# Expert items of a mixture layer run as big, small, big, small to the end, with overflow items in pairs behind them

## The reference

```python
def moe(h, router, w_gate_up, w_down):
    xt = h.reshape(B * S, D)                                  # 256 x 1024
    probs = jax.nn.softmax((xt @ router), axis=-1)            # 8 experts
    top_p, top_i = lax.top_k(probs, TOP_K)                    # 2 of 8
    top_p = top_p / jnp.sum(top_p, axis=-1, keepdims=True)
    gates = jnp.sum(one_hot(top_i, 8) * top_p[..., None], axis=1)
    y = jnp.zeros_like(xt)
    for e in range(N_EXPERTS):
        y = y + gates[:, e:e+1] * swiglu(xt, w_gate_up[e], w_down[e])
    return y
def swiglu(h, w_gate_up, w_down):                             # 1024 x 5632, 2816 x 1024
    g, u = jnp.split(h @ w_gate_up, 2, axis=-1)
    return (jax.nn.silu(g) * u) @ w_down
```

## Time and profile before

| | |
|---|---|
| Time, median of 3 | 1169.89 us (1169.28 to 1170.38) |
| Profiled execution, its time | 1167.88 us |
| Profiled execution, span | 1166.0 us |
| PE busy | 1089.2 us, 93% |
| DVE busy | 625.4 us, 54% |
| ACT busy | 522.0 us, 45% |
| Read from memory | 341.37 MB, 294 GB/s over the span |
| TensorE clock granted, mean | 0.979 of full |

### The profile page before, as it was taken

One profiled execution on the slowest core, in us unless ns is written; L12 is line 12 of the kernel. 1 busy time (PEld: TensorE's weight loads), 2 busy tenths in 40 slices (PEclk: granted clock), 3 DMA queues, 4 the chain that ended last, 5 costly groups with the idle time before them and its releaser, 6 DMA issues.

```text
span 1166.0 us, 15739 instructions
## 1 busy us (share of the span) xinstructions
PE 1089.2 (93%) x5708; PEld 800.3 (69%) x5708; DVE 625.4 (54%) x693; ACT 522.0 (45%) x571; POOL 22.5 (2%) x93
## 2 busy tenths in 40 slices
PE   7899999999999988999999999999998999999774
PEld 7867788888898777787446786446787788443131
DVE  6755555555654448895108894008886997301002
ACT  5544544344445644773016773016775676110001
POOL 2100000000000000000000000000000000000000
PEclk9889999999999999999999999999999999999998
DMA  9932455555454424997999999999999999799995
GB/s 353 335 108 86 165 184 184 177 186 211 145 182 147 140 73 146 370 361 270 379 409 409 400 410 396 391 409 410 400 409 367 343 361 357 287 403 409 406 403 202
DMA packets 122455, 343.47 MB, mean 295 GB/s; under 512 B 12893, under 2 KB 39562, under 8 KB 122378
## 3 DMA queue, kind: packets, MB, share of 16 engines
q1 hardware_dynamic: 122234, 341.94, 78.5%
q10 hardware_dynamic: 144, 0.52, 0.1%
HBM read 341.37 MB, written 1.05 MB: 294 GB/s over the span
## 4 chain that ended last, share of the span: by engine, by line
PE 75%; SPq 9%; DVE 5%; DMA 4%; issue 3%; ACT 3%; POOL 0%; POOLq 0%; DVEq 0%; ACTq 0%
PE ps L1454 19%; PE ps L1455 19%; PE ps L1456 19%; PE ps L1459 16%; SPq L361 5%; SPq L365 4%; DMA raw<-moe_w_gate_up_dram 3%; ACT whi L547 1%; DMA raw<-moe_w_down_dram 1%; DVE wlo L948 1%; PE ps L1789 1%; PE ps L1469 1%; DVE h L1131 1%; DVE wlo L937 0%; ACT xs L547 0%
## 5 line engine op out<-in xcount | busy, mean ns | idle before, releaser
L547 ACT ACTIVATE whi<-raw 128x2048 fp32r<-128x2048 f32 (+1 forms) x195 | 335.8, 1725 | 241.2 <-PE ps L1456 231.2
L948 DVE TENSOR_TENSOR wlo<-raw,whi 128x2048 fp32r<-128x2048 f32 x151 | 345.8, 2293 | 123.1 <-ACT whi L547 121.3
L1454 PE MATMUL ps<-whi,xhi 128*128 128x512 f32 (+3 forms) x688 | 265.7, 386 | 13.9 <-DVE wlo L948 5.1
L1455 PE MATMUL ps<-whi,xlo 128*128 128x512 f32 (+3 forms) x688 | 261.7, 380 | 0.0
L1456 PE MATMUL ps<-wlo,xhi 128*128 128x512 f32 (+3 forms) x688 | 261.3, 380 | 0.0
L1459 PE MATMUL ps<-raw,xs 128*64 128x512 f32 (+2 forms) x1024 | 158.5, 462 | 10.5 <-DMA raw<-moe_w_gate_up_dram 10.4
L1454 PEld LDWEIGHTS ps<-whi,xhi 128*128 128x128 f32 x688 | 131.1, 190 | 41.9 <-DVE wlo L948 7.4
L1456 PEld LDWEIGHTS ps<-wlo,xhi 128*128 128x128 f32 x688 | 130.9, 190 | 24.2
L1455 PEld LDWEIGHTS ps<-whi,xlo 128*128 128x128 f32 x688 | 130.9, 190 | 22.5
L1459 PEld LDWEIGHTS ps<-raw,xs 128*64 128x64 f32 x1024 | 67.1, 137 | 98.2 <-issue 65.6
L1454 PE MATMUL ps<-whi,hhi 128*128 128x512 f32 x264 | 106.5, 403 | 0.0
(11 more groups left out here) (282 smaller groups left out, 973.9 us busy)
## 6 DMA issues: line engine op xcount, KB each, us to landing
raw<-moe_w_gate_up_dram SPq DMA_DIRECT2D x256, 512.0 KB, 12.2
raw<-moe_w_down_dram SPq DMA_DIRECT2D x176, 512.0 KB, 14.0
raw<-moe_w_gate_up_dram SPq DMA_DIRECT2D x96, 384.0 KB, 9.5
raw<-ffn_w_gate_up_dram SPq DMA_DIRECT2D x44, 512.0 KB, 4.9
raw<-ffn_w_down_dram SPq DMA_DIRECT2D x22, 512.0 KB, 4.0
raw<-kv_shared_w_dram SPq DMA_DIRECT2D x16, 512.0 KB, 3.7
raw<-moe_w_gate_up_dram SPq DMA_DIRECT2D x32, 256.0 KB, 9.8
raw<-mla_w_o_dram SPq DMA_DIRECT2D x8, 512.0 KB, 14.0
```

The costliest lines, as they stand in the source:

```text
L547: return nc.scalar.activation(o, i, ACT.Copy, scale=scale)
L948: V.tensor_tensor(wlo[:, s, :].rearrange("p a w -> p (a w)"), raw[:, (hh // 2) % RAW, :], whi[:, s, :].bitcast(F32).rearrange("p a w -> p ...
L1454: pe.matmul(o, a_hi, b_hi, start=start, stop=False, skip_group_check=True)
L1455: pe.matmul(o, a_lo, b_hi, start=False, stop=False, skip_group_check=True)
```

## The change

The items now alternate to the end: B S B S B S B S. `PAIRS` becomes 4. Two pairs are still in straight code, then a loop over pairs follows, and the last pair is written out behind it. If there are overflow items, they follow in further pairs of one big and one small item; ITEMS grows from 13 to 14 rows. The number of further pairs, and which expert stands where in them, is worked out by DVE in a longer row of tiny operations. What an item does is unchanged, and so are its slots and which experts are small.

```diff
-NB = N_EXP - NS
-PAIRS = 2
-OVF = 5
-FIRST_OVF = 6
-LATE = FIRST_OVF + OVF
-ITEMS = LATE + 2
-ORDER = (0, 1, 5, 2, 6, 7) + OVF * (-1,) + (3, 4)
+PAIRS = N_EXP - NS
+OVF = 6
+FIRST_OVF = 2 * PAIRS
+ITEMS = FIRST_OVF + OVF
+ORDER = (0, 1, 5, 2, 6, 3, 7, 4) + OVF * (-1,)
...
             sp_eng.wait_ge(items_ready, 2)
-            for p in range(PAIRS):
+            for p in range(PAIRS - 2):
                 small_loads(p, at(2 * p + 1), lambda x: after_big(x, p))
                 big_loads(p + 1, at(2 * p + 2), lambda x: after_small(x, p))
-            final = sp_eng.value_load(final_i[0:1, 0:1], min_val=NB - 1, max_val=NB - 1 + OVF)
-            with sp_eng.Fori(PAIRS + 1, final + 1) as i:
-                big_loads(i, at(i + PAIRS), lambda x: after_big(x, i - 1))
-            small_loads(PAIRS, at(LATE), lambda x: after_big(x, final))
-            small_loads(PAIRS + 1, at(LATE + 1), lambda x: after_small(x, PAIRS))
+            final = sp_eng.value_load(final_i[0:1, 0:1], min_val=PAIRS - 1, max_val=PAIRS - 1 + OVF // 2)
+            with sp_eng.Fori(PAIRS - 2, final) as p:
+                small_loads(p, at(2 * p + 1), lambda x: after_big(x, p))
+                big_loads(p + 1, at(2 * p + 2), lambda x: after_small(x, p))
+            small_loads(final, at(2 * final + 1), lambda x: after_big(x, final))
...
-            for p in range(PAIRS):
+            for p in range(PAIRS - 2):
                 big(p, 2 * p, "small", p)
                 small(p, 2 * p + 1, "big", p + 1)
             pe.wait_ge(items_ready, 2)
-            final = pe.value_load(final_i[0:1, 0:1], min_val=NB - 1, max_val=NB - 1 + OVF)
-            with pe.Fori(PAIRS, final) as i:
-                big(i, i + PAIRS, "big", i + 1)
-            big(final, final + PAIRS, "small", PAIRS)
-            small(PAIRS, final + PAIRS + 1, "small", PAIRS + 1)
-            small(PAIRS + 1, final + PAIRS + 2, None, None)
+            final = pe.value_load(final_i[0:1, 0:1], min_val=PAIRS - 1, max_val=PAIRS - 1 + OVF // 2)
+            with pe.Fori(PAIRS - 2, final) as p:
+                big(p, 2 * p, "small", p)
+                small(p, 2 * p + 1, "big", p + 1)
+            big(final, 2 * final, "small", final)
+            small(final, 2 * final + 1, None, None)
```

ACT and DVE get the same loop, and POOL's runs over the same number of items. In the routing, seven instructions on DVE (lines 1390 to 1396) become twenty:

```diff
+            V.tensor_scalar(cap2[:, :], place[:, :], 0.5, None, ALU.is_gt)
+            step(V.tensor_scalar(wide[:, :], place[:, :], NS + 0.5, None, ALU.is_gt))
+            step(V.tensor_tensor(wide[:, :], cap2[:, :], wide[:, :], ALU.is_equal))
+            step(V.tensor_scalar(cap[:, :], wide[:, :], -float(P - SMALL), -float(SMALL), ALU.mult, ALU.add))
             step(V.tensor_tensor(ovf[:, :], cnt[:, :], cap[:, :], ALU.add))
             step(V.tensor_scalar(ovf[:, :], ovf[:, :], 0.0, None, ALU.is_gt))
+            step(V.tensor_tensor(wide[:, :], wide[:, :], ovf[:, :], ALU.mult))
+            step(V.tensor_tensor(cap2[:, :], ovf[:, :], wide[:, :], ALU.subtract))
+            V.tensor_tensor_scan(csum[:, :], ones[:, 0:N_EXP], wide[:, :], 0.0, ALU.mult, ALU.add)
+            step(V.tensor_tensor_scan(csum2[:, :], ones[:, 0:N_EXP], cap2[:, :], 0.0, ALU.mult, ALU.add))
...
+            step(V.tensor_tensor(csum[:, :], csum[:, :], cap2[:, :], ALU.add))
...
-            V.tensor_scalar(final_i[:, :], csum[:, N_EXP - 1:N_EXP], float(NB - 1), None, ALU.add).then_inc(items_ready, 1)
+            V.tensor_scalar(final_i[:, :], extra[:, 2:3], float(PAIRS - 1), None, ALU.add).then_inc(items_ready, 1)
```

More of the change, by code:

```diff
@@ L208, in build @@
             ("sp", [P, HEADS, 384], F32))
-        lg, lg2, oh1, oh2, sc8, msk, gates, posn, posc, ovf, csum, key, place, cap, cap2, less, order, oh, prod, \
+        lg, lg2, oh1, oh2, sc8, msk, gates, posn, posc, ovf, csum, key, place, cap, cap2, wide, csum2, extra, less, order, oh, prod, \
             m1, m2, den, best, rank, cnt, tf, xr = over(
@@ L901, in _ @@
             act.wait_ge(items_ready, 2)
[L902 to L910, removed]
+            final = act.value_load(final_i[0:1, 0:1], min_val=PAIRS - 1, max_val=PAIRS - 1 + OVF // 2)
+            with act.Fori(PAIRS - 2, final) as p:
+                big(p, 2 * p, "small")
+                small(p, 2 * p + 1, "big")
+            big(final, 2 * final, "small")
+            small(final, 2 * final + 1, None)
+            n_items = 2 * final + 2
             for c in range(TC):
@@ L1204, in add_in, with big @@
                                                op0=ALU.mult, op1=ALU.add).then_inc(h_ready[4], 1)
-            def big(i, g, row, following, next_row):
+            def big(i, g, following):
                 def gate(j):
@@ L1226, in big @@
                     if x == 14:
-                        item_gates(g, row)
-                        choose(g + 1, next_row, following)
+                        item_gates(g)
+                        choose(g + 1, following)
                     if x == FU - 1:
@@ L1243, in big, with small @@
                 add_in(g)
-            def small(p, g, row, following, next_row):
+            def small(p, g, following):
                 def gate(j):
@@ new lines, in _ @@
+            step(V.tensor_scalar(extra[:, 2:3], n_narrow, 2.5, None, ALU.is_gt))
+            step(V.tensor_tensor(extra[:, 1:2], extra[:, 1:2], extra[:, 2:3], ALU.add))
+            V.tensor_tensor(extra[:, 1:2], extra[:, 1:2], n_wide, ALU.max)
+            step(V.scalar_tensor_tensor(out=cap2[:, :], in0=csum2[:, :], scalar=extra[:, 0:1], in1=csum2[:, :],
+                                        op0=ALU.mult, op1=ALU.add))
+            V.scalar_tensor_tensor(out=extra[:, 2:3], in0=n_narrow, scalar=extra[:, 0:1], in1=extra[:, 1:2],
+                                   op0=ALU.mult, op1=ALU.max)
@@ L1427, in _ @@
                 split_low_unit(H_MOE + 2 * x)
-            for p in range(PAIRS):
-                big(p, 2 * p, 2 * p, "small", 2 * p + 1)
-                small(p, 2 * p + 1, 2 * p + 1, "big", 2 * p + 2)
+            for p in range(PAIRS - 2):
+                big(p, 2 * p, "small")
+                small(p, 2 * p + 1, "big")
             dve.wait_ge(items_ready, 2)
-            final = dve.value_load(final_i[0:1, 0:1], min_val=NB - 1, max_val=NB - 1 + OVF)
-            with dve.Fori(PAIRS, final) as i:
-                big(i, i + PAIRS, i + PAIRS, "big", i + PAIRS + 1)
-            big(final, final + PAIRS, final + PAIRS, "small", LATE)
-            small(PAIRS, final + PAIRS + 1, LATE, "small", LATE + 1)
-            small(PAIRS + 1, final + PAIRS + 2, LATE + 1, None, None)
-            n_items = final + PAIRS + 3
+            final = dve.value_load(final_i[0:1, 0:1], min_val=PAIRS - 1, max_val=PAIRS - 1 + OVF // 2)
+            with dve.Fori(PAIRS - 2, final) as p:
+                big(p, 2 * p, "small")
+                small(p, 2 * p + 1, "big")
+            big(final, 2 * final, "small")
+            small(final, 2 * final + 1, None)
+            n_items = 2 * final + 2
             dve.wait_ge(gbc_in, 16)
```

32 lines of the change are left out of this document (16 added, 16 removed).

## The result

| | before | after |
|---|---|---|
| Time, median of 4 | 1169.74 us (1169.28 to 1170.38) | 1151.6 us (1151.32 to 1153.6) |
| Ratio, with its 95% interval | | 0.9848 (0.9831 to 0.9865) |
| Profiled execution, its time (span) | 1167.88 (1166.0) us | 1151.79 (1150.0) us |
| PE, DVE, ACT busy | 1089.2, 625.4, 522.0 us | 1085.4, 627.3, 522.4 us |
| Read from memory | 341.37 MB | 341.37 MB |

The account below looks back on a forecast made before the run. PE was taken to bound the kernel, with S3 slowed by an emptied weight ring. Terms -18.4 and +0.5 gave -17.9 from the profiled 1167.88: 1150.0, plus 2.0 for the median, 1152.0 us; range 1147.5 to 1158.

Parts of the forecast that it names:

- Steps 1 and 3: Mixture stretches: S2, moved behind a big item, takes 62.2 us; B2 and B3 take 110.96 us each, as B1 did.
- step 3: Handovers between items: B2 and B3 together take 221.92 us against 216.93 before, a cost of 5.0 us.
- step 2: Last small item, S3, with no next gather: 62.3 us, bounds 58.5 and 75, its end set by the last unit's landing.
- step 4: The mixture behind S1's end: 346.4 us in place of 364.84, so 18.4 us less.
- signs named: Profile after: S3 62 us with hardly any PE waits for transfers, last `ys` at some 1134.5, B0's first product at most 1 us late.
- step 5: Longer DVE routing ahead of B0: partly absorbed by DVE's idle time, delaying PE's first product by 0 to 0.8 us, taken as 0.5.
- step 6: Loops on each engine, with computed waits and addresses: no cost, at most 0.5 us a handover, 1 us in all.
- The ring is not refilled: Rival, chance 0.09: later pairs run slower in transfers, so S2 and S3 begin with fewer units: 1158 to 1164 us.
- The transfers bind throughout: Rival, chance 0.03 (no change): S3's wait comes back in pieces before S2, B3 and S3: 1170 us.
- SP's issue as a bound: Rival, chance 0.03 (slower): SP's issue of computed transfers for S2 and B3 becomes the bound: 1178 to 1193 us.
- More is gained: Rival, chance 0.05: the last item's missing gather counts in full and transfers keep S0's state: 1147 to 1149 us.

Follow-up runs that it names:

- e1: The kernel after with its items in the order B B S S B S B S: 1172.16 us, ratio 1.0005 to the kernel before.
- e2: The kernel before with the order B B B B S S S S: 1209.75 us, ratio 1.0335.
- e9: The kernel before with each weight transfer of the last small item half as wide, same computing: 1146.37 us, ratio 0.9793 to the kernel before.
- e10: The kernel after with each weight transfer of the last small item half as wide, same computing: 1146.51 us, ratio 0.9794 to the kernel before.
- e3: The kernel after with thirteen of the added DVE instructions of the routing taken out again: 1152.43 us, ratio 0.9856 to the kernel before.
- e6: The kernel after with the loop written out on all five engines and a fixed number of rounds: 1152.88 us, ratio 0.9843 to the kernel before.
- e5: The kernel after with a gather, its result thrown away, put back into the last small item: 1151.74 us, ratio 0.9842 to the kernel before.
- e11: The kernel after, PE taking three units of the following small item behind the big item's ninth down unit and two more in `begin`: 1144.49 us, ratio 0.9791.
- e7: The kernel after with 2.1 MB more transfers per small item, ahead of its units 2 and 8, while the big item runs: 1163.21 us, ratio 0.9939.
- e8: The kernel after with 2.1 MB more transfers per small item, ahead of its units 18 and 24, while the small item runs: 1170.61 us, ratio 1.0003.
- e4: The kernel after with 24 more DVE instructions in the routing, each waiting for the one before: 1157.82 us, ratio 0.9896 to the kernel before.

## Why the prediction was right

I forecast 1152.0 us, in a range from 1147.5 to 1158; it was 1151.6, by the mechanism named.

**Steps 1 and 3 held as numbers.** S2 was put at 62.2 and took 62.05. B2 and B3 were put at 110.96 each and took 110.95 and 111.04. e1, e2 and e9 show that the reading behind them is the cause, and not only fits it: the loss goes with the place behind a small item, comes once for each such place, and vanishes with the last item's transfers.

**But they are right only together.** The prediction says of the four small items that PE's work in them is the same. In the stretches as cut it is not: S3 before holds 363 products and S3 after 345, while B2 and B3 together hold 987 before and 1006 after. The 24 us between 85.97 and 62 contain the 4.8 of PE's work that e9 and e10 price, and the 5.0 of step 3 is not a cost of handovers but this work on the other side of the cuts. The empty ring cost 18 to 20 us, not 24. Both steps went by the same cuts, so the sum came out right.

**S3 (step 2)** was the one term that was mis-sized: 62.3 forecast, 62.97 measured, and 63.1 to 64.5 in e1 and e3 to e6. The argument from the last landing was right, as the five units at 2.55 and e5 show, but I took S1's landing for S3's. That S3's last unit lands at the end of a pair with little slack, so that each small delay of the transfers ahead arrives there, would explain the spread; no run separates it.

**The sum (step 4)**: 18.4 less behind S1's end was forecast, 17.83 measured. The missing 0.6 is S3's. Two of the signs named did not come out as written: the last `ys` is at 1136.56 and not some 1134.5, and PE still waits 4.3 us for transfers in S3.

**The routing (step 5)** was put at 0.5. Counted from `rt_cnt` it is 0.56 at PE's transposes, and 0.42 at the end of B0 (554.37 less 439.75, against 552.36 less 438.16). `final_i` came 2.08 later, and the idle time of DVE behind it took 1.4 of this, much as the step said: where the earlier trace rows have 1.15 and 0.66 of waiting, after has 0 and 0.38. From the end of the kernel after's routing:

```profile
445.62 0.15 DVE L1419 TENSOR_SCALAR final_i<-rt_extra 128x1 int32<-128x1 f32 x1
445.68 1.12 DVE L1172 SCALAR_TENSOR_TENSOR xlo<-ps,gcol,xhi 128x128 fp32r<-128x128 f32 x4
447.18 1.13 DVE L1172 SCALAR_TENSOR_TENSOR xlo<-ps,gcol,xhi 128x128 fp32r<-128x128 f32 x4 [0.38 <-ACT xhi L545]
```

What the prediction did not have is that `rt_cnt` itself is 1.59 later in the profiled execution of after. That is not of the change, since the code ahead of it is the same: by 225 us (a group of `h` in the dense layer) 1.47 of it was there (226.43, not 224.96), with a granted clock of 0.86 from 50 to 100 us where it had been 0.90, and e3 to e6, e10 and e11 have this group at 225.2 to 226.8. With 0.42 from the routing and 0.17 won in S0 to S1 it makes the 1.84 at S1's end. It also puts the transposes ahead of B0 2.15 later in the trace, past the 1 us that the prediction allowed, though the change accounts for 0.56 of it. So single executions differ by some 1.5 us ahead of the mixture, and the profiled difference (16.1) is 2.0 below that of the medians (18.1). My number for the profiled execution, 1150.0, was 1.8 too low; the 2.0 that I had added for the median made up for it, since after was profiled at its median (1151.79 and 1151.6) and before was not. That the forecast is within 0.4 us is luck to this extent.

**The loops (step 6)** were put at nothing, and the stretches of e6 show nothing.

**The rivals.** *The ring is not refilled* did not happen, but of the two arguments for and against it the wrong one decided. I held SP's 14.7 us of waiting for DVE against it, and e7 shows that this waiting is no room. The slack of 1.5 us in a pair, which I had worked out from the lengths, was the right one: e7 finds 0.6 to 1.7. The rival's mechanism was nearer than its chance of 0.09 says: e7, with 5.2 us more of transfers for each small item, took the 1158 to 1164 that I had given for it. *The transfers bind throughout* falls with the result; e8 shows what it would have looked like. *SP's issue as a bound* falls: S2 and B3 took what S1 and B2 took, and SP still waited 14.7 to 18.1 us for slots. *More is gained* falls for the reason that e5 gives.

On bandwidth the prediction quoted one figure of the Trainium skill too narrowly. "DMA: Bandwidth & Descriptors" gives 358 GB/s in its Specifications, but says under Measured that this is the share of a core when both cores of a pair stream, and "Perfetto Trace Analysis" (Roofline) adds that one core alone is bounded by its DMA engines at some 435. This kernel runs on one core, and the items from S0 to B3 show 395 to 404 GB/s, up to 408 in e7, so the second statement agrees with the trace and the rival drawn from the first was none.

## What to carry to other kernels

Cut the timeline at the ends of like pieces of work and put length and GB/s side by side: a piece that is slow only in one place of the order, next to a piece that moves less than full pace, is a case for exchanging the two. "Perfetto Trace Analysis" of the Trainium skill (Optimization Strategy) says the same of stretches with different limits, that they may gain from being interleaved; here, with a buffer of a third of an item, each small item behind a small one cost 18 to 20 us. Look at what lies on either side of a cut before you give a difference to a wait: two stretches of the same item can hold different work. Read the room of the transfers from GB/s against the highest seen, in pieces of a few us, and not from the sum of the issuing engine's waits; then, when a pair is near the pace of transfers, ask for the slots to be freed sooner, as e11 does.

## What the runs showed of the hardware

Waits of the issuing engine for DVE fell from 14.9 to 0.7 us in B1 of e7, and all its waits there from 21.8 to 6.7, while the rate only rose from 403 to 408 GB/s: a queue that paused often moved hardly less. Where two long pauses (5.0 and 6.2 us) had only 4 transfers between them, the rate did fall, to 316 to 365 GB/s for 15 us; with 10 transfers between pauses as long (5.0 and 6.6, e11) it stayed at 388 to 404.

The granted clock behind the routing was not the same in all kernels. In the kernel after, and in e4:

```profile
446.00:450.00 4.00, 1.64 (x5) 1.45 (x6) 3.56 (x12) 1.52 (x5) 0.45 (x1) 0.75 0.02 6
450.00:454.00 4.00, 4.00 (x16) 3.17 (x16) 3.48 (x16) 0.93 (x1) 0.16 (x1) 0.83 0.78 248
454.00:458.00 4.00, 4.00 (x20) 3.30 (x18) 3.63 (x7) 2.90 (x2) 0.00 (x0) 1.00 0.04 14
```

```profile
454.00:458.00 4.00, 4.00 (x11) 3.13 (x10) 3.48 (x16) 0.00 (x0) 0.01 (x1) 0.52 0.79 231
458.00:462.00 4.00, 4.00 (x19) 3.26 (x19) 2.87 (x6) 3.04 (x2) 0.00 (x0) 1.00 0.08 31
```

In e4, where PE had stood 6.67 us before its transposes, 4.00 busy us hold 11 products at 0.52, near the lower of the two levels (1.2 GHz), and 19 at full clock (2.4 GHz) right behind. By PE's timeline 12 products behind the transposes follow each other at 0.43 us and the later ones at 0.23; in the kernel after it is 6. Six more at 0.20 each are the 1.2 us of its cost that the delay does not explain. The kernel after has the lower level in a part of the 8 us from 446 on; before and e3 had 1.00 there. At 456.01 before, PE waited 1.15 for DVE's `wlo`; after, this wait is gone, so the slower products used time that would have been idle. Why the clock stayed low in after and not in e3 no run here tells: PE's idle time ahead of the transposes is the same in both (2.39 and 2.40).
